# Two pad tensors between the buffers of a two-block transformer kernel on one core: activations and their split forms begin at a multiple of 256 bytes

## The chip, the cores and the metric

The kernel runs on one core of a Trainium2 chip. The metric is the device time of one execution in microseconds, as the median of the runs. A core has five engines with instruction streams of their own: TensorE (rows PE for matmuls and PEld for weight loads), VectorE (DVE), ScalarE (ACT), GpSimd (POOL) and SyncE (SP), which issues the DMAs here. The memory of the core that the engines read is called SBUF; each of its 128 partitions holds a line of bytes, and every tensor of the kernel lies at one byte address that is the same in all partitions.

## The reference

`reference()` computes two transformer blocks, each of depth two, over 512 tokens of width 1024, in float32:

```python
# first block, twice
x = layer_norm(ALPHA * x + 0.5 * swiglu(x, w_in, w_out))      # 1024 -> 2 x 2816 -> 1024
x = layer_norm(ALPHA * x + mixer(x))     # mLSTM, then windowed attention
x = layer_norm(ALPHA * x + 0.5 * swiglu(x, w_in, w_out))
# second block, twice
h = h + concat(hgrn2(p), nsa(p)) @ w_out           # p = rms_norm(h) @ w_in
h = h + swiglu(rms_norm(h), w_ffn_in, w_ffn_out)   # 1024 -> 2 x 2816 -> 1024
def swiglu(x, w_in, w_out):
    gu = x @ w_in; g, u = gu[..., :D_FF], gu[..., D_FF:]
    return (silu(g) * u) @ w_out
```

There are thus six swiglu layers, and most of the arithmetic is in them.

## The kernel before

**Weights.** All weights come as 535 units of 128 x 1024 float32, fetched in order into four buffers `raw0..3` (`Chip.fetch`). Each unit is split into a high part, rounded to the fp32r format, by ScalarE (`Chip.hi`, L211, into `whi0..3`), and the rest, by VectorE (`Chip.lo`, L219, into `wlo0..3`). Activations are split likewise: `xh` and `xl`, each 8 blocks of 128 channels by 512 tokens. A product of weights and activations is three matmuls in fp32r: high by high, high by low, low by high.

**A matmul** has a stationary operand of 128 x 128, loaded by a weight load of its own, and a moving operand of 256 or 512 columns. In a row of the profile the moving operand stands first: `ps<-tz,whi` moves tz past whi.

**A swiglu layer** (`Ffn`, six of them, `hf`, `tz`, `es` and `fb` are its tensors) has these stages:

1. Blocks j = 0 to 3 of the 22 blocks of 128 hidden channels: whole products with 256 or 512 moving columns of `xh` and `xl`, stationary `whi` and `wlo` (`Chip.three`, L238 to L240).
2. Blocks j = 4 to 21 (`seven_t`, `product`, L792 to L794): seven products of half size take the place of eight. Each is 12 matmuls with 256 moving columns, so a block is 84 matmuls. Three of the seven move a quarter of the activations (`xh`, `xl`), four move a form of the tokens T1 to T4, a sum or difference of quarters, that lies in `tz`. The stationary operand is a form of the weights, made by VectorE (`sum_v`) in `es` and `fb` and split into `whi` and `wlo` (L892, L987). There are 18 such blocks in a layer, 108 in all, and 9072 of these matmuls.
3. The product with `w_out` (`Norm.tile_t`, L367 to L369): the weights move (512 columns of `whi` or `wlo`), and the stationary operand is a 128 x 128 piece of the hidden activations, split into the ring `tz` (`split_a`, `split_v`, L920, L927).

**The mixers** take tensors of their own in the bytes that `hf`, `tz`, `es` and `fb` have in the swiglu layers. Their projections either move `xh` and `xl` (L238 to L240) or move the weights with `xh` and `xl` stationary (`Chip.wide`, L246 to L248; L1269 to L1271; L2118 to L2120; L1653 to L1655), their output products move the weights (L367 to L369). The compression in the second block moves the weights past `nxh` and `nxl`, whose pieces have 62 columns (L2132 to L2134).

**Where tensors lie.** Tensors are laid out in the order in which they are declared, each start rounded up to 32 bytes. The starts in the built program, as the remainder by 256 bytes:

| tensors | remainder before |
|---|---|
| raw, whi, wlo, xr, xh, xl | 128 |
| res, tmp, rows, st | 192 |
| hf, tz, es, fb | 64 |
| mixers: q and k of all three, nv, hkq, hv, had, hao, nkc | 64 |
| nxh | 0 (its pieces: 0, 248, 240, ...) |

The pieces of xh, xl, whi, wlo and tz that one matmul reads begin at multiples of 512 bytes behind the tensor's start, so they have its remainder.

Of the kernel before, what the change touches and what calls it, by code (L numbers as in the profile page):

```python
# [7 lines left out]
P = 128  # L8
# [94 lines left out]
class Tally:  # L103
# [4 lines left out]
    def __init__(self, make):  # L108
        self.make, self.sems, self.value, self.n = make, {}, {}, {}
        self.known = False  # L110
# [53 lines left out]
class Chip:  # L164


    def __init__(self, nc, ctx, xin, xtin, wst, vec, row, tab, mats_in, gain, out):
        self.nc, self.xin, self.xtin, self.wst, self.vec, self.row, self.tab = nc, xin, xtin, wst, vec, row, tab
        self.mats_in, self.gain, self.out = mats_in, gain, out
        self.tally = Tally(lambda name: ctx.enter_context(nc.semaphore(name)))  # L170
        self.up, self.at, self.also = self.tally.up, self.tally.at, self.tally.also
        sb = self.sb = lambda name, shape, dt=F32, scope=ctx: scope.enter_context(nc.sbuf_tensor(name, shape, dt))
        self.ps = ctx.enter_context(nc.psum_tensor("ps", [P, 8, 512], F32))
        self.raw = [sb(f"raw{i}", [P, UT * P]) for i in range(NRAW)]
        self.whi = [sb(f"whi{i}", [P, UT * P], F32R) for i in range(NW)]
        self.wlo = [sb(f"wlo{i}", [P, UT * P], F32R) for i in range(NW)]
        self.xr = sb("xr", [P, 4, D])
        self.xh = sb("xh", [P, KD, T], F32R)
        self.xl = sb("xl", [P, KD, T], F32R)
        self.vc = sb("vc", [P, V_N])  # L180
        self.res = sb("res", [P, P])
        self.ident = self.res[:, :]
        self.tmps = sb("tmp", [P, 5, T])
        self.tmp = [self.tmps[:, i, :] for i in range(5)]
        self.z = [self.tmps[:, 2 * i:2 * i + 2, :].rearrange("p a n -> p (a n)") for i in range(2)]
        self.rows = sb("rows", [P, 2, D])
        self.st = sb("st", [P, 4, 24])
        self.n_units = wst.shape[0]
        self.freed, self.read = {}, {}
# [2852 lines left out]
```

How the kernel before makes its waits and increments, by code:

```python
    def hi(self, a, upto):  # L204
        while self.nhi <= min(upto, self.n_units - 1):
            u = self.nhi
            a.wait_ge(*self.at(f"raw{u % NRAW}", u))
            if u >= NW:
                a.wait_ge(*self.at(*self.freed.get(u, ("gemm", "unit", u - NW))))
            a.activation(self.whi[u % NW][:, :], self.raw[u % NRAW][:, :], COPY).then_inc(*self.up("whi", u))
            self.nhi += 1
# [1 line left out]
    def lo(self, v, upto):  # L214
        while self.nlo <= min(upto, self.n_units - 1):
            u = self.nlo
            v.wait_ge(*self.at("whi", u))
            v.tensor_tensor(self.wlo[u % NW][:, :], self.raw[u % NRAW][:, :], f32(self.whi[u % NW][:, :]), SUB).then_inc(*self.up("wlo", u))
            self.nlo += 1
# [1 line left out]
    def fetch(self, s, u):  # L222
        if u >= NRAW:
            s.wait_ge(*self.at(*self.read.get(u - NRAW, ("wlo", u - NRAW))))
        s.dma_start(self.raw[u % NRAW][:, :], self.wst[u, :, :]).then_inc(*self.up(f"raw{u % NRAW}", u, by=16))
# [23 lines left out]
    def project(self, t, u, b, ks):  # L250
        if 0 in ks:
            t.wait_ge(*self.at("wlo", u))
        for k in ks:
            ins = self.three(t, self.bank(b), u, k, self.xh[:, k, :], self.xl[:, k, :], k == 0, k == KD - 1)
            if k == KD - 1:
                ins.then_inc(*self.up("gemm", "unit", u))
# [23 lines left out]
    def scalar(self, a):  # L281
# [6 lines left out]
            if k == 5:  # L288
                c.hi(a, 1)
        a.wait_ge(*c.at("vcin"))
# [1 line left out]
    def vector(self, v):  # L292
# [5 lines left out]
            if k == 5:  # L298
                c.lo(v, 1)
        v.wait_ge(*c.at("vcin"))
```

## Time and profile before

| what | value |
|---|---|
| median of 3 runs | 3289.93 us (3289.71 to 3290.17) |
| the profiled execution, its own time | 3290.32 us |
| its span, first to last instruction | 3288.5 us |
| TensorE matmuls | 22750, busy 3197.6 us (97%) |
| VectorE busy | 2144.5 us (65%) |
| ScalarE busy | 1534.5 us (47%) |
| DMA | 331.55 MB, mean 101 GB/s |

Busy time counts an engine as busy when any of its instructions is under way. A matmul's duration in a row includes the way through the array, which overlaps with the next matmul; what one matmul costs in a chain is its pitch, the time from its start to the start of the next. The pitch can be read from the timeline: the starts of two matmuls, some places apart, and their number between.

### The profile page before, as it was taken

What the parts mean: (1) busy time and instruction counts of PE and PEld (TensorE: products, weight loads), DVE (VectorE), ACT (ScalarE), POOL (GpSimd) and SP (SyncE); (2) the same over time, 40 slices, a digit from 0 to 9 for tenths busy, and PEclk for the clock granted to TensorE, in tenths of its full rate; (3) what the DMA queues carried; (4) which work ended last, traced back from release to release, by engine and by line L of the source; (5) the groups of instructions that cost most, each with busy time, mean ns of one, the idle gap of its engine ahead of it and who ended that gap; (6) DMA issues with size and microseconds to landing.
All of it is one profiled execution on the core that took longest, in us unless ns stands there. A gap on an engine that the chain in (4) does not pass through costs nothing. (4 is left out here: it accounts for less than half of the span.)

```text
span 3288.5 us, 55994 instructions
## 1 busy us (share of the span) xinstructions
PE 3197.6 (97%) x22750; PEld 2829.6 (86%) x22750; DVE 2144.5 (65%) x3383; ACT 1534.5 (47%) x2651; POOL 136.3 (4%) x144
## 2 busy tenths in 40 slices
PE   9999999999999999999999988999999989999999
PEld 8998888899889988768998776779998767789987
DVE  6875544787577766447875766557774665567863
ACT  4553444355434543553554544444554444444553
POOL 0000111000000001000000100000000000000000
PEclk9999999999999999999999999999999999999999
DMA  4443222234323432112343221113442221123332
GB/s 177 133 141 114 94 71 86 79 129 144 122 86 114 141 117 98 52 65 84 129 142 117 89 77 59 34 65 112 133 142 96 97 65 53 40 87 113 139 125 71
DMA packets 104512, 331.55 MB, mean 101 GB/s; under 512 B 11264, under 2 KB 16640, under 8 KB 104256
## 3 DMA queue, kind: packets, MB, share of 16 engines
q1 hardware_dynamic: 104256, 327.96, 29.7%
q8 instruction: 182, 2.98, 0.4%
q14 instruction: 74, 0.61, 0.1%
HBM read 325.69 MB, written 2.23 MB: 100 GB/s over the span
## 5 line engine op out<-in xcount | busy, mean ns | idle before, releaser
L219 DVE TENSOR_TENSOR wlo<-raw,whi 128x1024 fp32r<-128x1024 f32 x319 | 388.0, 1225 | 441.7 <-ACT whi L211 441.2
L211 ACT ACTIVATE whi<-raw 128x1024 fp32r<-128x1024 f32 x319 | 334.0, 1054 | 391.2 <-PE ps L369 338.6
L792 PE MATMUL ps<-tz,whi 128*128 128x256 f32 x1728 | 479.9, 278 | 3.4 <-ACT tmp L964 3.4
L793 PE MATMUL ps<-tz,whi 128*128 128x256 f32 x1728 | 478.5, 277 | 0.0
L794 PE MATMUL ps<-tz,wlo 128*128 128x256 f32 x1728 | 477.7, 276 | 0.0
L369 PE MATMUL ps<-whi,tz 128*128 128x512 f32 x1056 | 416.0, 394 | 0.0
L368 PE MATMUL ps<-wlo,tz 128*128 128x512 f32 x1056 | 413.8, 392 | 0.0
L367 PE MATMUL ps<-whi,tz 128*128 128x512 f32 x1056 | 411.3, 390 | 0.0
L794 PE MATMUL ps<-xh,wlo 128*128 128x256 f32 x1296 | 365.7, 282 | 0.0
L792 PE MATMUL ps<-xh,whi 128*128 128x256 f32 x1296 | 365.3, 282 | 0.0
L793 PE MATMUL ps<-xl,whi 128*128 128x256 f32 x1296 | 364.3, 281 | 0.0
L238 PE MATMUL ps<-xh,whi 128*128 128x512 f32 (+1 forms) x936 | 332.8, 356 | 18.2 <-DVE wlo L219 10.8
L792 PEld LDWEIGHTS ps<-tz,whi 128*128 128x128 f32 x1728 | 325.3, 188 | 4.4 <-issue 4.4
L793 PEld LDWEIGHTS ps<-tz,whi 128*128 128x128 f32 x1728 | 325.3, 188 | 0.0
L794 PEld LDWEIGHTS ps<-tz,wlo 128*128 128x128 f32 x1728 | 324.7, 188 | 0.0
L240 PE MATMUL ps<-xh,wlo 128*128 128x512 f32 (+1 forms) x936 | 320.3, 342 | 0.0
L239 PE MATMUL ps<-xl,whi 128*128 128x512 f32 (+1 forms) x936 | 320.2, 342 | 0.0
L792 PEld LDWEIGHTS ps<-xh,whi 128*128 128x128 f32 x1296 | 246.1, 190 | 0.5
L794 PEld LDWEIGHTS ps<-xh,wlo 128*128 128x128 f32 x1296 | 246.3, 190 | 0.0
L793 PEld LDWEIGHTS ps<-xl,whi 128*128 128x128 f32 x1296 | 246.1, 190 | 0.3
L368 PEld LDWEIGHTS ps<-wlo,tz 128*128 128x128 f32 x1056 | 198.3, 188 | 45.1
L367 PEld LDWEIGHTS ps<-whi,tz 128*128 128x128 f32 x1056 | 198.3, 188 | 43.1
(348 smaller groups left out, 6417.9 us busy)
## 6 DMA issues: line engine op xcount, KB each, us to landing
raw<-in_w SPq DMA_DIRECT2D x535, 512.0 KB, 4.0
fb<-in_w SPq DMA_DIRECT2D x108, 256.0 KB, 2.6
rows<-in_row SPq DMA_DIRECT2D x15, 512.0 KB, 4.9
xr<-in_xt SPq DMA_DIRECT2D x4, 512.0 KB, 6.8
xr<-in_x SPq DMA_DIRECT2D x1, 2048.0 KB, 7.8
mn<-bounds SPq DMA_DIRECT2D x8, 256.0 KB, 4.4
out<-tmp SPq DMA_DIRECT2D x4, 256.0 KB, 3.0
out<-rows SPq DMA_DIRECT2D x4, 256.0 KB, 2.3
```

What stands on the lines that cost most here:

```text
L211: a.activation(self.whi[u % NW][:, :], self.raw[u % NRAW][:, :], COPY).then_inc(*self.up("whi", u))
L219: v.tensor_tensor(self.wlo[u % NW][:, :], self.raw[u % NRAW][:, :], f32(self.whi[u % NW][:, :]), SUB).then_inc(*self.up("wlo", u))
L238: t.matmul(out, wh, xh, start=first, stop=False)
L239: t.matmul(out, wh, xl, start=False, stop=False)
L240: return t.matmul(out, wl, xh, start=False, stop=last)
L367: t.matmul(b, xh[:, sl], wh, start=k == 0, stop=False)
L368: t.matmul(b, xh[:, sl], wl, start=False, stop=False)
L369: ins = t.matmul(b, xl[:, sl], wh, start=False, stop=k == self.k - 1)
L792: t.matmul(out, fh[:, sl], xh[:, k, :], start=first and k == 0, stop=False, skip_group_check=not first)
L793: t.matmul(out, fh[:, sl], xl[:, k, :], start=False, stop=False, skip_group_check=not first)
L794: ins = t.matmul(out, fl[:, sl], xh[:, k, :], start=False, stop=k == 3, skip_group_check=not first)
```

## The change

Two tensors that nothing reads or writes are declared, one of 128 bytes ahead of `xh` and one of 64 bytes behind `xl`. No instruction is added, removed or moved.

```diff
         self.xr = sb("xr", [P, 4, D])
+        sb("pad0", [P, 32])
         self.xh = sb("xh", [P, KD, T], F32R)
         self.xl = sb("xl", [P, KD, T], F32R)
+        sb("pad1", [P, 16])
         self.vc = sb("vc", [P, V_N])
```

What follows from the order of declaration: `xh` and `xl` go up by 128 bytes, everything behind them by 192. The remainders by 256 become 0 for `xh`, `xl`, `hf`, `tz`, `es`, `fb` and for the mixers' q, k and others that had 64; 128 for `res`, `tmp`, `rows` and `st`; 192 for `nxh`. `raw`, `whi`, `wlo` and `xr` stay at 128.

## Rows read from the trace of the kernel before

**Rows 1.** The page: share of the span of each engine, and the slices.
```profile
span 3288.5 us, 55994 instructions
PE 3197.6 (97%) x22750; PEld 2829.6 (86%) x22750; DVE 2144.5 (65%) x3383; ACT 1534.5 (47%) x2651; POOL 136.3 (4%) x144
PE   9999999999999999999999988999999989999999
PEclk9999999999999999999999999999999999999999
```

**Rows 2.** Groups by line and form: busy us, mean ns | idle before.
```profile
L792 PE MATMUL ps<-tz,whi 128*128 128x256 f32 x1728 | 479.9, 278 | 3.4 <-ACT tmp L964 3.4
...
L369 PE MATMUL ps<-whi,tz 128*128 128x512 f32 x1056 | 416.0, 394 | 0.0
...
L792 PE MATMUL ps<-xh,whi 128*128 128x256 f32 x1296 | 365.3, 282 | 0.0
...
L238 PE MATMUL ps<-xh,whi 128*128 128x512 f32 x488 | 203.8, 418 | 11.9 <-DVE xl L297 7.1 <-DVE wlo L219 4.6 <-ACT wv L1725 0.2
...
L238 PE MATMUL ps<-xh,whi 128*128 128x256 f32 x448 | 128.9, 288 | 6.3 <-DVE wlo L219 6.2
```

**Rows 3.** Timeline, PE, a product that moves tz: start us, us.
```profile
694.65 0.28 PE L792 MATMUL ps<-tz,whi 128*128 128x256 f32 x1
...
697.03 0.28 PE L792 MATMUL ps<-tz,whi 128*128 128x256 f32 x1
```

**Rows 4.** Timeline, PE, a product that moves xh and xl.
```profile
682.31 0.28 PE L794 MATMUL ps<-xh,wlo 128*128 128x256 f32 x1
...
683.51 0.29 PE L792 MATMUL ps<-tz,whi 128*128 128x256 f32 x1
```

**Rows 5.** Timeline, PE, 512 moving columns of xh and xl.
```profile
50.07 0.39 PE L238 MATMUL ps<-xh,whi 128*128 128x512 f32 x1
...
51.43 0.39 PE L238 MATMUL ps<-xh,whi 128*128 128x512 f32 x1
```

**Rows 6.** Timeline, PE, 512 moving columns of weights, tz stationary.
```profile
299.65 0.39 PE L367 MATMUL ps<-whi,tz 128*128 128x512 f32 x1
...
305.14 0.39 PE L367 MATMUL ps<-whi,tz 128*128 128x512 f32 x1
```

**Rows 7.** Timeline, PE, 256 moving columns of weights, xh and xl stationary.
```profile
450.38 0.28 PE L1271 MATMUL ps<-whi,xl 128*128 128x256 f32 x1
...
451.58 0.28 PE L1269 MATMUL ps<-whi,xh 128*128 128x256 f32 x1
```

**Rows 8.** Timeline, PE, weights moving, nxh and nxl stationary: first and last pieces.
```profile
1918.07 0.28 PE L2132 MATMUL ps<-whi,nxh 128*62 128x256 f32 x1
...
1919.36 0.28 PE L2134 MATMUL ps<-whi,nxl 128*62 128x256 f32 x1
...
1925.89 0.28 PE L2133 MATMUL ps<-wlo,nxh 128*62 128x256 f32 x1
...
1927.07 0.28 PE L2134 MATMUL ps<-whi,nxl 128*62 128x256 f32 x1
```

**Rows 9.** Timeline, PEld, chains of weight loads with short matmuls.
```profile
1971.31 0.97 PEld L2247 LDWEIGHTS ps<-nkc,nq 128*128 128x128 f32 x8
1834.55 1.86 PEld L430 LDWEIGHTS ps<-tmp,xr 128*128 128x128 f32 x16 [0.25 <-issue]
```

**Rows 10.** Timeline, PE, and line L1291: 512 columns at two cycles each.
```profile
447.85 1.02 PE L1291 MATMUL ps<-mq,mk 128*128 128x512 f32 x2
L1291 PE MATMUL ps<-mq,mk x32: 590/591/592, 401.6 to 518.4; 128*128 128x512 f32 x32
```

**Rows 11.** Timeline, DVE, one block of stage 2 and the next block's first row.
```profile
693.47 0.43 DVE L1037 SCALAR_TENSOR_TENSOR ps<-tmp,ps 128x256 f32<-128x256 f32 x1 [0.65 <-PE ps L794]
...
696.28 0.69 DVE L1023 TENSOR_TENSOR hf<-tmp,ps 128x512 f32<-128x512 f32 x1 [1.25 <-PE ps L794]
696.88 1.22 DVE L987 TENSOR_TENSOR wlo<-es,whi 128x1024 fp32r<-128x1024 f32 x1
...
703.23 0.43 DVE L1037 SCALAR_TENSOR_TENSOR ps<-tmp,ps 128x256 f32<-128x256 f32 x1 [0.65 <-PE ps L794]
```

**Rows 12.** Timeline, PE, the second product of the next block begins.
```profile
698.79 0.29 PE L792 MATMUL ps<-tz,whi 128*128 128x256 f32 x1
```

**Rows 13.** Windows, stage 2 of one layer: busy us (x instructions), granted clock.
```profile
652.00:820.00 168.00, 167.44 (x1440) 167.27 (x1439) 133.26 (x186) 90.16 (x139) 0.00 (x0) 1.00 0.40 136
```

**Rows 14.** Line L987 on DVE: duration ns min/median/max, by source.
```profile
L987 DVE TENSOR_TENSOR wlo<-raw,whi x108: 1218/1219/1226, 45.4 to 3143.5; 128x1024 fp32r<-128x1024 f32 x108
L987 DVE TENSOR_TENSOR wlo<-fb,whi x108: 1215/1216/1218, 62.2 to 3158.5; 128x1024 fp32r<-128x1024 f32 x108
```

## The prediction

> **What bounds the kernel now.** I read the page first. TensorE is busy 97% of the span, at full granted clock in nearly every slice, and VectorE is at 65% [rows 1]. The groups by line say what TensorE does: its long groups have hardly any idle time before them [rows 2]. But the busy time of overlapping matmuls says nothing of what one costs, so I went to the timeline for pitches. A stretch of the stage with the seven products is 168 us with 1440 matmuls and 0.6 us without one [rows 13]. What a matmul costs from start to start is thus what the kernel costs, and a change of addresses can act only there.
>
> **Pitches by place.** The granted clock is 1.00 in that stretch, the level of 2.4 GHz, so 256 columns at one per cycle are 106.7 ns and 512 are 213.3 ns. Read off the timeline:
>
> Moving tz (remainder 64), stationary whi or wlo (128): 2.38 us over 21 matmuls, 113.3 ns, 6.7 above the columns [rows 3]. Moving xh or xl (128), the same stationary operand: 1.20 us over 10, 120.0 ns, 13.3 above [rows 4]. 512 columns of xh or xl: 1.36 us over 6, 226.7 ns, also 13.3 above [rows 5]. Weights moving (128) with xh stationary (128): 1.20 us over 10, 120.0 ns [rows 7]. Weights moving with tz stationary (64), 512 columns: 5.49 us over 24, 228.8 ns, 15.4 above [rows 6]. Weights moving with nxh stationary, whose pieces lie at 0, 248, 240 and so on: 1.29 us over 11, 117.3 ns for the first pieces, 1.18 us over 10, 118 ns for the last [rows 8].
>
> Rows 3 and 4 are the same instruction, with the same stationary operand, in the same stage. They differ in the moving operand's place, and the excess is 16 cycles at remainder 64 and 32 cycles at 128: a quarter of a cycle for each byte past a multiple of 256, as if a stream began at the multiple and dropped what it did not need. It is 32 cycles at 512 columns as well, so it is paid once per matmul. I take this as my theory: the moving operand's remainder by 256 sets the excess, and at 0 it is gone.
>
> **A floor.** A matmul also needs its weight load. Chains with little to move show what a chain of loads costs: 8 loads span 0.97 us, less the last one's 0.19 that is 0.78 over 7; 16 span 1.86 us, 1.67 over 15: 111.4 and 111.3 ns [rows 9]. The stationary operands there lie at 64 and at 128, so this floor does not depend on their place between these. I take 111.5 ns for 256 columns. With 512 columns the load has room. The nearest row for a wide matmul free of the excess is L1291, which takes two cycles per column: two of them span 1.02 us, less one duration of 0.59 is 0.43 us against 0.427 of columns [rows 10]. So 1 to 3 ns remain, and I take 216 ns.
>
> **The change part by part.**
>
> 1. Stage 2 of the swiglu layers. VectorE repeats its block every 703.23 - 693.47 = 9.76 us [rows 11], and a block is 84 matmuls: 116.2 ns on average, transitions between the two kinds included. At 111.5 ns a block is 9.37 us. 9072 matmuls x 4.7 ns = 42.6 us less. Bounds: at 113.3, if zero is no better than tz's 64, 26.3 us less; at the columns alone, 106.7, 86.2 us less, which the loads' floor excludes if it holds for this format too.
> 2. Moving xh and xl with 256 columns outside stage 2: 3 x 448 = 1344 matmuls [rows 2], 120.0 to 111.5: 11.4 us less. Bounds: 9.0 and 17.9.
> 3. Moving xh and xl with 512 columns: 3 x 488 = 1464 [rows 2], of which the first 48 of the kernel wait for their data anyway, so about 1416 x 10.7 = 15.2 us less. Bounds: nothing, and 13.3 each or 18.8.
> 4. Weights moving past tz (stage 3), 3 x 1056 = 3168 [rows 2, 6]. The moving side stays at 128, so its 13.3 stay. The stationary side goes from 64 to 0. At 128 it costs nothing on top (226.7), at 64 it costs 2.1. At 0 it may cost nothing (6.6 us less) or, if it grows with the distance, 4.2 (6.6 us more). I take no change. The other wide matmuls that move weights, 1152 of them, have xh stationary at 128 and go to 0: nothing, or up to 4.2 ns, 4.8 us more. The 62-column pieces go down from 0 by 8 bytes each to 136 and show no excess that follows their place [rows 8]; I take zero here too.
> 5. VectorE and ScalarE read and write the moved tensors. Source at 128 and at 64 give 1219 and 1216 ns for the same operation [rows 14]; nothing. The fp32 matmuls of the mixers pay about 1 to 5 ns at any remainder; nothing.
>
> Would another engine take over in stage 2? VectorE waits 0.65 + 1.25 = 1.90 us in a block of 9.76 [rows 11], so its own work needs 7.86 us and a block of 9.37 covers it. Its tightest hand-over is the second split: gate at the end of a product, 0.69 and 1.22 us, done at 698.10, needed by the second product of the next block at 698.79 [rows 11, 12]. Two products lie between, which shrink by some 0.1 us. The cover holds, and would be gone only near 8.6 us a block.
>
> The sum: 42.6 + 11.4 + 15.2 = 69.2 us less. The profiled execution itself took 3290.32 us for a span of 3288.5; its time is 0.4 us above the median, so both bases give the same: 3221.
>
> **A rule that speaks against it.** The Trainium skill, "SBUF — State Buffer", section "SBUF: two separate sides", says that TensorE's reads never wait for another engine; by that the places would not matter and the time would stay. Rows 3 and 4 differ by 6.7 ns with nothing else changed, so if it holds for other engines, TensorE's own two streams are still sensitive to place. "TensorE: Matmul & The Clock Gate" of the Trainium skill, section "Wait — 56ns, not 53.3ns?", has a fixed 2.5 ns on top of the columns whatever the addresses: 109.2 and 215.8 ns as an estimate. The wide figure fits my 216; the narrow one would give 9072 x 7.0 + 1344 x 10.8 + 16 = 94 us less, 3196, but rows 9 put the loads above it.
>
> **Rivals.**
>
> *Partial (0.17).* Zero is as good as 64 but no better: 26.3 + 9.0 + 1416 x 6.7 = 9.5, 45 us less: 3245. For it: rows 3 are only 1.8 ns above the loads' floor, so they don't prove that 64 costs 16 cycles rather than something else. Against: the round 16 and 32.
>
> *Mutual distance (0.09).* What costs is that the two streams lie at the same remainder; 128 apart, both are free, whichever moves. Then the matmuls that move weights gain as well: 3168 x 12.8 + 1152 x 10.7 + 1632 narrow ones x 8.5 = 67 us on top: 3154. Against it: the stationary pieces of nxh go from 128 apart from the moving weights to 8 apart, at 117 and 118 ns [rows 8].
>
> *Period of 128 (0.09), the one on the other side.* The excess depends on the remainder by 128, so 0 is as bad as 128, and tz had the best place. Then xh and xl stay at 120 and tz joins them: a block becomes 84 x 120 = 10.08 us, 0.32 x 108 = 34.6 us more; stage 3's stationary side gets 6.6 back: 28 us more, 3318. For it: no fp32r row moves anything at 0. It decides if the moving tz shows 117 ns or more.
>
> *Nothing (0.06).* The difference of rows 3 and 4 comes from something other than the start, such as the strides or the far address: 3290.
>
> **How the numbers follow.** My forecast has 0.59, the others as given. The likeliest one's own range is 3200 to 3236: less 11 us for the stationary side and a floor at 113 in part, more for a floor near 109. A measurement here tells 0.2%, 6.6 us, from no change. The range for 8 in 10 takes in the partial case and leaves out most of mutual distance and both on the other side: 3180 to 3262. Faster: 0.59 + 0.17 + 0.09 = 0.85; within 0.2%: 0.06; slower: 0.09.
>
> **What the profile of the changed kernel would show.** A product moving tz and one moving xh at the same pitch, 111 to 112 ns, and no transitions between them; VectorE's block at 9.37 us, its waits for TensorE shorter by 0.39; L238 with 512 columns at 216 ns; stage 3 at 227 to 231. The prediction is wrong if the moving side's place is not what made 113 and 120, if a stationary operand at 0 costs stage 3 more than 4 ns a matmul, or if the loads' floor is another one with whi at 128 than in rows 9.

## The result and the profile after

The changed kernel takes 3329.17 us in the median of 4 runs (3326.75 to 3329.40), the kernel before in the same comparison 3290.05 us (3289.71 to 3290.61). The ratio is 1.0117, with a 95% interval of 1.0100 to 1.0135: the change costs 39 us. The forecast was 3221 us, 69 us less than before.

The head of the page and two groups by line of the changed kernel; lines behind the pads are two higher, so L794 to L796 were L792 to L794, and L369 was L367.

```profile
span 3327.6 us, 55994 instructions
PE 3237.2 (97%) x22750; PEld 2851.6 (86%) x22750; DVE 2144.8 (64%) x3383; ACT 1534.5 (46%) x2651; POOL 136.7 (4%) x144
```

```profile
L794 PE MATMUL ps<-tz,whi 128*128 128x256 f32 x1728 | 486.7, 282 | 3.4 <-ACT tmp L966 3.4
...
L794 PE MATMUL ps<-xh,whi 128*128 128x256 f32 x1296 | 364.7, 281 | 0.0
```

The instructions are the same, and no idle time came up in front of these matmuls; VectorE and ScalarE are as busy as before [rows 1, 2]. In mean duration the matmuls that move tz went from 278 to 282 ns. The pitch says more. The timeline of TensorE in the changed kernel, in pairs of rows that are 21, 10, 24 and 24 matmuls apart: moving tz, moving xh, 512 columns of xh, and stage 3.

```profile
790.32 0.28 PE L794 MATMUL ps<-tz,whi 128*128 128x256 f32 x1
...
792.81 0.28 PE L794 MATMUL ps<-tz,whi 128*128 128x256 f32 x1
...
727.67 0.28 PE L794 MATMUL ps<-xh,whi 128*128 128x256 f32 x1
...
728.85 0.28 PE L795 MATMUL ps<-xl,whi 128*128 128x256 f32 x1
...
638.63 0.39 PE L240 MATMUL ps<-xh,whi 128*128 128x512 f32 x1
...
644.23 0.39 PE L240 MATMUL ps<-xh,whi 128*128 128x512 f32 x1
...
852.61 0.40 PE L369 MATMUL ps<-whi,tz 128*128 128x512 f32 x1
...
858.19 0.39 PE L369 MATMUL ps<-whi,tz 128*128 128x512 f32 x1
```

In each pair the start of the second less the start of the first, by the number of matmuls between, is the pitch: 2.49 us over 21, 118.6 ns, where [rows 3] had 113.3; 118 where [rows 4] had 120.0; 5.60 over 24, 233.3, where [rows 5] had 226.7; and 5.58 over 24, 232.5, where [rows 6] had 228.8. VectorE, which waits for TensorE once in each block of stage 2 at this line, shows the block:

```profile
709.36 0.43 DVE L1039 SCALAR_TENSOR_TENSOR ps<-tmp,ps 128x256 f32<-128x256 f32 x1 [0.75 <-PE ps L796]
...
712.27 0.69 DVE L1025 TENSOR_TENSOR hf<-tmp,ps 128x512 f32<-128x512 f32 x1 [1.36 <-PE ps L796]
...
719.32 0.43 DVE L1039 SCALAR_TENSOR_TENSOR ps<-tmp,ps 128x256 f32<-128x256 f32 x1 [0.75 <-PE ps L796]
```

A block takes 9.96 us instead of 9.76 and VectorE waits 2.11 us in it instead of 1.90 [rows 11]. The granted clock was not lower. It is at 1.00 in the window of [rows 13] here too (the window begins some us earlier in the layer than it did before, so its counts don't compare):

```profile
652.00:820.00 168.00, 167.44 (x1397) 166.57 (x1396) 129.58 (x182) 86.34 (x133) 0.00 (x0) 1.00 0.37 131
```

**Is it the other engines?** VectorE and ScalarE read and write the moved tensors too and might get in TensorE's way. A stretch of the swiglu layer in which VectorE, ScalarE, GpSimd and the DMA do nothing answers that. Here it is in the kernel before and then in the changed one, each time as a window (busy time of PE, PEld, DVE, ACT and POOL, granted clock, DMA share, GB/s) and as two matmuls in it, 22 apart:

```profile
644.60:649.70 5.10, 5.10 (x24) 4.24 (x23) 0.00 (x0) 0.00 (x0) 0.00 (x0) 1.00 0.00 0
644.59 0.39 PE L240 MATMUL ps<-xh,wlo 128*128 128x512 f32 x1
...
649.57 0.39 PE L238 MATMUL ps<-xh,whi 128*128 128x512 f32 x1
```

```profile
649.60:654.80 5.20, 5.20 (x24) 4.20 (x23) 0.00 (x0) 0.00 (x0) 0.00 (x0) 1.00 0.00 0
649.59 0.40 PE L242 MATMUL ps<-xh,wlo 128*128 128x512 f32 x1
...
654.73 0.40 PE L240 MATMUL ps<-xh,whi 128*128 128x512 f32 x1
```

The 22 matmuls take 4.98 us and 5.14 us. With the trace's full digits that is 226.7 and 233.3 ns each, so the whole difference is there while nothing but TensorE works. In stage 3 it is the same: where VectorE and ScalarE are both idle, the mean pitch went from 228.8 to 232.6 ns. Moving tz, TensorE is never alone for long, but where only ScalarE works beside it the pitch went from 113.4 to 118.6. What is left are TensorE's own reads.

**Where the 39 us are.** The time from the start of each matmul to the start of the next, summed over the whole trace by what moves and what is stationary, after less before, waits included: tz moving, 5184 matmuls, +23.0 us (115.1 to 119.6 ns each); stage 3 with tz stationary, 3168, +10.6; 512 columns of xh, 1464, +3.7; weights moving past xh with 512 columns, 1152, +3.4; 256 columns of xh, 5244 (the 12 of L812 counted in), -3.5; all others together, +1.7. The sum is 38.9 us, and 33.6 of it are in the matmuls that have tz on one side. How far such a sum varies with nothing changed in the pitches can be seen below, where all tensors go up by 128: up to 1.7 us for one kind.

### The profile page after: what moved, and what is told of

It reads as the page before. It is cut to its first block and busy times, and to the rows that moved or that the text cites. A ratio compares the mean times of both kernels' runs of the same rounds, so it can differ in the third digit from the quotient of the medians.

```text
span 3327.6 us, 55994 instructions
## 1 busy us (share of the span) xinstructions
PE 3237.2 (97%) x22750; PEld 2851.6 (86%) x22750; DVE 2144.8 (64%) x3383; ACT 1534.5 (46%) x2651; POOL 136.7 (4%) x144
## 5 line engine op out<-in xcount | busy, mean ns | idle before, releaser
L794 PE MATMUL ps<-tz,whi 128*128 128x256 f32 x1728 | 486.7, 282 | 3.4 <-ACT tmp L966 3.4
L796 PE MATMUL ps<-tz,wlo 128*128 128x256 f32 x1728 | 486.3, 281 | 0.0
L795 PE MATMUL ps<-tz,whi 128*128 128x256 f32 x1728 | 486.2, 281 | 0.0
L369 PE MATMUL ps<-whi,tz 128*128 128x512 f32 x1056 | 417.7, 396 | 0.0
L794 PE MATMUL ps<-xh,whi 128*128 128x256 f32 x1296 | 364.7, 281 | 0.0
L796 PE MATMUL ps<-xh,wlo 128*128 128x256 f32 x1296 | 364.6, 281 | 0.0
L794 PEld LDWEIGHTS ps<-tz,whi 128*128 128x128 f32 x1728 | 325.2, 188 | 4.5 <-issue 4.5
L796 PEld LDWEIGHTS ps<-tz,wlo 128*128 128x128 f32 x1728 | 325.2, 188 | 0.0
L794 PEld LDWEIGHTS ps<-xh,whi 128*128 128x128 f32 x1296 | 243.9, 188 | 0.5
L796 PEld LDWEIGHTS ps<-xh,wlo 128*128 128x128 f32 x1296 | 243.9, 188 | 0.0
```

Source lines behind the costliest of these rows:

```text
L369: t.matmul(b, xh[:, sl], wh, start=k == 0, stop=False)
L794: t.matmul(out, fh[:, sl], xh[:, k, :], start=first and k == 0, stop=False, skip_group_check=not first)
L795: t.matmul(out, fh[:, sl], xl[:, k, :], start=False, stop=False, skip_group_check=not first)
L796: ins = t.matmul(out, fl[:, sl], xh[:, k, :], start=False, stop=k == 3, skip_group_check=not first)
```

## The experiments

All of them are the kernel before with other pads, so an edit is given by its pads and by the remainders by 256 that it makes (weights, xh and xl, tz and all behind it). Before is 128, 128, 64; the change is 128, 0, 0. Each ratio is to runs of the kernel before on the same chip. Of two theories at the start, M says that the distance between the two operands counts, A that the place of the moving one does.

**All tensors up by 128 (0, 0, 192).**

```diff
+        sb("padr", [P, 32])
         self.raw = [sb(f"raw{i}", [P, UT * P]) for i in range(NRAW)]
```

> One pad of 128 bytes ahead of raw: every tensor goes up by 128 bytes, so whi, wlo, xh and xl lie at remainder 0 by 256 and tz at 192, and all distances between tensors stay. Theory M (the distance between the moving and the stationary operand by 256 bytes sets the pitch): nothing changes, 3290 us, tz moving at 113.3 ns, xh moving at 120.0, wide matmuls at 226.7 and 228.8. Theory A (the place of the moving operand by 256 bytes sets it, with 0 as bad as in the changed kernel): xh moving at 119 with a spread instead of a fixed 120, wide ones at 232, some 3300 to 3330 us.

Measured: 3290.22 us, ratio 1.0001 (0.9992 to 1.0010). Timeline of TensorE in this kernel, moving tz, moving xh, and stage 3:

```profile
780.59 0.28 PE L793 MATMUL ps<-tz,whi 128*128 128x256 f32 x1
...
782.97 0.28 PE L793 MATMUL ps<-tz,whi 128*128 128x256 f32 x1
...
719.21 0.28 PE L793 MATMUL ps<-xh,whi 128*128 128x256 f32 x1
...
720.41 0.28 PE L794 MATMUL ps<-xl,whi 128*128 128x256 f32 x1
...
841.66 0.39 PE L368 MATMUL ps<-whi,tz 128*128 128x512 f32 x1
...
847.15 0.39 PE L368 MATMUL ps<-whi,tz 128*128 128x512 f32 x1
```

113.3, 120.0 and 228.8 ns, as before to the tenth. xh moves from a multiple of 256 here and costs the full 13.3 ns above its columns, so theory A, and with it the theory of the prediction, is false. A theory of places by themselves that repeats every 128 bytes would also see nothing in this run. It fails in the next ones: xh goes from 128 to 0, and its pitch with 512 columns from 226.7 to 233. Shifts of all tensors by less than 128 were not tried.

**xh and xl alone (128, 0, 64).**

```diff
+        sb("pad0", [P, 32])
         self.xh = sb("xh", [P, KD, T], F32R)
         self.xl = sb("xl", [P, KD, T], F32R)
+        sb("pad1", [P, 32])
```

> xh and xl go to remainder 0, as in the change, and tz and all behind it keep 64. The changed kernel shows tz moving at 119 ns (113.3 to 115 before) and xh moving at 118.7. Theory M: tz stays at 113.3 to 115, stage 3 stays at 228.8, only the matmuls with xh change: 1464 + 1152 wide ones by about 3 to 5 ns, 9 us more in all, narrow ones about 1 ns less, 5 us less: 3290 to 3298 us. Theory A says the same of it. A third one, that the total order of the tensors or their far address counts, would show tz changed as well.

Measured: 3306.56 us, ratio 1.0053 (1.0036 to 1.0070). More than either theory gave. Stage 3 stays, but tz moving does not, though its remainder and that of its weights did not change:

```profile
785.78 0.28 PE L794 MATMUL ps<-tz,whi 128*128 128x256 f32 x1
...
788.25 0.28 PE L794 MATMUL ps<-tz,whi 128*128 128x256 f32 x1
...
847.50 0.39 PE L369 MATMUL ps<-whi,tz 128*128 128x512 f32 x1
...
853.00 0.39 PE L369 MATMUL ps<-whi,tz 128*128 128x512 f32 x1
```

2.47 us over 21, 117.6 ns, and as steady as the 113.3 was: over all layers nine in ten of these pitches lie from 117 to 119 ns. tz did go up by exactly 256 bytes here, but that is not the reason: it went up by the same 256 in three kernels below ((128, 64, 64), xl alone and (128, 96, 64)), and there it is at 113.3. At one and the same distance there are two lasting rhythms. The slow one costs 12.7 us in this kernel, the sum over tz moving.

**tz and all behind it alone (128, 128, 0).**

```diff
         self.xl = sb("xl", [P, KD, T], F32R)
+        sb("pad1", [P, 48])
```

> xh and xl keep 128, tz and all behind it go to remainder 0. Both theories: tz moving at 119 ns instead of 114.5, 5184 x 4.4 = 23 us more, and stage 3 at 232 instead of 228.8, 10 us more: 3320 to 3325 us, that is most of what the change costs.

Measured: 3324.11 us, ratio 1.0109 (1.0094 to 1.0124), as expected: tz moving +23.5 us, stage 3 +10.7, and xh stays at 120.0 and 226.7. In its timeline tz moving, then stage 3:

```profile
790.94 0.28 PE L793 MATMUL ps<-tz,whi 128*128 128x256 f32 x1
...
793.43 0.28 PE L793 MATMUL ps<-tz,whi 128*128 128x256 f32 x1
...
853.31 0.39 PE L368 MATMUL ps<-whi,tz 128*128 128x512 f32 x1
...
858.88 0.40 PE L368 MATMUL ps<-whi,tz 128*128 128x512 f32 x1
```

This half of the change makes 34 of its 39 us. Stage 3's weights did not move either: here it is the stationary operand's place relative to them that changed the pitch.

**xh, xl and tz all at 64 (128, 64, 64).**

```diff
+        sb("pad0", [P, 48])
         self.xh = sb("xh", [P, KD, T], F32R)
         self.xl = sb("xl", [P, KD, T], F32R)
+        sb("pad1", [P, 16])
```

> xh and xl go to remainder 64, where tz lies, 64 below the weights. Theories M and A: xh moving falls from 120.0 to 113.3 ns in narrow matmuls (5232 of them, 30 to 35 us less, and the transitions between tz and xh vanish, some 5 us less), wide ones with xh moving or stationary go from 226.7 to about 229 (2600 of them, 6 us more): 3255 to 3265 us. A theory in which tz is fast for another reason than its place would leave xh at 120 and the time at 3290.

Measured: 3261.55 us, ratio 0.9915 (0.9900 to 0.9929), faster than both kernels. tz has gone up by 256 bytes in all and keeps its 113.3. In its timeline moving xh, then 512 columns of xh:

```profile
712.46 0.28 PE L794 MATMUL ps<-xh,whi 128*128 128x256 f32 x1
...
713.60 0.28 PE L795 MATMUL ps<-xl,whi 128*128 128x256 f32 x1
...
626.61 0.39 PE L240 MATMUL ps<-xh,whi 128*128 128x512 f32 x1
...
632.21 0.39 PE L240 MATMUL ps<-xh,whi 128*128 128x512 f32 x1
```

xh moving falls to 1.14 us over 10, 114 ns (29.1 us less over all), and the transitions between the two kinds are gone (tz 4.3 us less). With 512 columns it rises from 226.7 to 233.3 (8.1 us more): what is the best place for 256 columns is a bad one for 512. That was expected at 229, from stage 3; but there the weights move past tz and lie 64 above it, here xh moves and lies 64 below. The sign counts.

**Other distances.** Three more layouts, each with two new ones: (128, 96, 32), (128, 192, 160), (128, 224, 192), by pads ahead of xh and behind xl of 56 and 0, 16 and 8, 24 and 8 elements.

> xh and xl at remainder 96, 32 below the weights' 128; tz and all behind at 32, 96 below. A theory of two kinds of place (a distance that is a whole number of 64-byte pieces or not): both get the same narrow pitch. A theory of a smooth dependence between the known points (0: 120.0, 64 below: 113.3, 128: 119): xh at 116 to 117 and tz at 116, time about 3290. If 64 below is a sharp optimum, both are at 119 to 120 and the time is above 3300.

> xh and xl at 192, 64 above the weights; tz and all behind at 160, 32 above. If only the size of the distance counts: xh moving at 113.3 ns as with 64 below, and wide ones as in rows of 64 below. If the sign counts (the stream that is ahead): xh near 119 to 120. Stage 3 then has the weights 32 below tz: between 226.7 (distance 0) and 232 (distance 128).

> xh and xl at 224, 96 above the weights; tz and all behind at 192, 64 above, so that in stage 3 the moving weights lie 64 below tz. A sign that counts: tz moving in stage 2 slower than 113.3, and stage 3 other than the 228.8 of 64 above. Only the size: 113.3 and 228.8 as before, with xh at 116 to 119.

Measured: 3320.50 (1.0092, 1.0063 to 1.0121), 3297.52 (1.0026, 1.0014 to 1.0037) and 3334.23 us (1.0134, 1.0104 to 1.0163). In the first, the time is that of the sharp optimum, and the pitches, 118.1 and 117.4, lie between it and the smooth curve. In the second and third the sign counts, but 64 above is better than was expected of it, 115.2 for 119 to 120. Pitches from all runs, each the mean over the matmuls of one kind that follow at least twelve of the same, in ns:

| moving less stationary, bytes | 256 columns | 512 columns |
|---|---|---|
| 0 | 120.0 | 226.7 |
| -32 | 118.1 | 233.3 |
| +32 | 116.7 | 233.3 |
| -64 | 113.3 to 113.9, or 117.7 | 233.3 |
| +64 | 115.2, or 117.8 | 228.9 to 230.3, or 233.0 |
| -96 | 117.4 | 234.2 |
| +96 | 120.0 | 233.3 |
| 128 | 118.7 | 232.4 to 232.9 |

For 512 columns the same place as the stationary operand is best and all others cost 2 to 7.5 ns, most of them 6 or 7. For 256 columns the same place is the worst or nearly so, and 64 below, in its fast rhythm, is the best. At 0 every run that has this distance shows the same fixed pitch; at 128 the pitch with 256 columns wanders between 115 and 122.

**wlo alone, xl alone.** In a triple the first and second matmul have whi stationary, the third wlo; while the second runs, wlo is loaded. These two ask which pair of operands it is that collides. (The first pad moves xr with wlo; both leave the remainder of tz at 64.)

```diff
+        sb("padw", [P, 16])
         self.wlo = [sb(f"wlo{i}", [P, UT * P], F32R) for i in range(NW)]
         self.xr = sb("xr", [P, 4, D])
+        sb("pad0", [P, 48])
```

> wlo alone goes 64 bytes up to 192; whi, xh, xl at 128, tz at 64. In each triple the first and second matmul have whi stationary and the third wlo; while the second runs, the load of wlo for the third runs. Theory N (the moving stream collides with the load for the next matmul, which runs under it): the second matmul of a triple changes, in wide ones of xh and xl L239's successor in pitch, from 226.7 to 229 to 233, L238 and the last one stay. Theory O (a matmul depends on its own stationary operand): the third changes and the second stays. In narrow ones moving xh a drop from 120 toward 113 for the one that changes. Time between 3285 and 3300.

```diff
         self.xh = sb("xh", [P, KD, T], F32R)
+        sb("padm", [P, 48])
         self.xl = sb("xl", [P, KD, T], F32R)
+        sb("pad1", [P, 16])
```

> xl alone goes to 64; xh, whi and wlo stay at 128, tz at 64. Only the second matmul of a triple has another distance (its own stationary whi and the load of wlo under it both 64 above the stream). This gives the lag between a matmul whose stream is moved and the row whose pitch changes: no lag, then in wide matmuls the pitch that starts at the xl row is the one near 233 to 236; a lag of one, then it is the wlo row's. With wlo moved alone the wlo row had 235.8. With a lag of one that points at the load of wlo under the second matmul's stream (theory N), with no lag at the third's own stationary operand (theory O). Time 3290 to 3320.

Measured: 3316.36 us (1.0080, 1.0050 to 1.0109) and 3284.57 us (0.9981, 0.9970 to 0.9991). The mean pitches with 512 columns, for the three of a triple in order, are 226.8, 226.6, 226.7 before; 228.4, 229.1, 235.8 with wlo moved; 229.3, 229.2, 228.4 with xl moved. The sum over a triple is 680, 693 and 687 ns, against 700 with all at 64. With wlo moved, 9.1 of the 13 ns stand at the third matmul; with xl moved the 7 ns are spread over all three. So neither theory N nor O is shown: it stays open whether the stream meets the load under it or a matmul depends on its own stationary operand. Both times lie outside what was expected. With wlo moved, the distance of tz to wlo changed as well, which the expectation left out: tz moving costs 20.4 us more and stage 3 9.9. With xl moved, xh and xl with 256 columns gain 8.0 us.

**xh and xl at 96, tz at 64 (128, 96, 64).** What leads tz into the slow rhythm?

```diff
+        sb("pad0", [P, 56])
         self.xh = sb("xh", [P, KD, T], F32R)
         self.xl = sb("xl", [P, KD, T], F32R)
+        sb("pad1", [P, 8])
```

> xh and xl at 96, tz and all behind at 64, 64 below the weights. With xh moved alone to 0, tz ran at a fixed 117.7 ns in its unchanged place, with xh at 128 or 64 at a fixed 113.3. Theory H (64 apart there are two lasting rhythms, 113.3 and 117.7, and the product before decides which one is taken; a product whose own pitch drifts, as xh does at 0 and at 96, leads into the slow one): tz at 117.7, time about 3305 to 3310. Theory K (only xh at a distance of 128 does that, for a reason of its own): tz at 113.3 to 114, xh at 117 to 118 as measured with 96 before, wide xh at 233.3: 3285 to 3290 us.

Measured: 3309.89 us, ratio 1.0069 (1.0052 to 1.0085). The time is theory H's, the pitches of tz, of xh (118.1) and of the wide matmuls of xh (233.3) are theory K's. In its timeline tz moving, then stage 3:

```profile
783.57 0.28 PE L794 MATMUL ps<-tz,whi 128*128 128x256 f32 x1
...
785.95 0.28 PE L794 MATMUL ps<-tz,whi 128*128 128x256 f32 x1
...
844.93 0.40 PE L369 MATMUL ps<-whi,tz 128*128 128x512 f32 x1
...
850.53 0.40 PE L369 MATMUL ps<-whi,tz 128*128 128x512 f32 x1
```

tz is at 113.3, so a drifting product ahead does not by itself bring the slow rhythm. But stage 3, with both operands at the remainders of the kernel before, is at 233.3 instead of 228.8, in all six layers, and costs 12.1 us. Its weights and tz lie at the very addresses that they have in the kernel (128, 64, 64), and there it costs what it did before. So the second rhythm exists with 512 columns too, and the distance by 256 bytes does not alone decide which one is taken. What does, these runs don't tell.

**Wide matmuls of xh cut in two.** With xh at 64 and, as a control, in the kernel before:

```diff
         wh, wl = self.w(u, j)
-        t.matmul(out, wh, xh, start=first, stop=False)
-        t.matmul(out, wh, xl, start=False, stop=False)
-        return t.matmul(out, wl, xh, start=False, stop=last)
+        n = xh.shape[-1]
+        for a in range(0, n, HT):
+            o, h, l = (x[:, a:a + HT] for x in (out, xh, xl))
+            t.matmul(o, wh, h, start=first and a == 0, stop=False)
+            t.matmul(o, wh, l, start=False, stop=False)
+            ins = t.matmul(o, wl, h, start=False, stop=last and a + HT >= n)
+        return ins
```

> As with xh, xl, tz all at 64, and each wide matmul of xh or xl past a weight is cut in two of 256 columns (1464 become 2928, with as many more weight loads). The wide ones cost 233.3 ns there, two narrow ones at 113.3 to 114 cost 227 to 228: 1416 x 5.5 = 8 us less than 3261.6, 3253 us. If the extra loads or instructions cost more than the columns, 3262 or above.

> The same cut in the kernel before, where xh and xl lie with the weights: two narrow ones at 120.0 take the place of one wide at 226.7, 13.3 ns x 1416 = 19 us more: 3309. It is the counterpart of the cut with xh at 64: the same edit with the other sign, by the place alone.

Measured: 3268.12 us (0.9941, 0.9924 to 0.9957) with xh at 64, the single runs from 3254.53 to 3274.33; 3302.88 us (1.0040, 1.0025 to 1.0055) in the kernel before. The profiled execution of the first was its fastest, 3254.53 us, and there the forecast is met; a stretch of the former wide matmuls in its timeline, ten apart:

```profile
601.04 0.28 PE L243 MATMUL ps<-xh,whi 128*128 128x256 f32 x1
...
602.18 0.28 PE L244 MATMUL ps<-xl,whi 128*128 128x256 f32 x1
```

114 ns each, 228 for a pair, against 233.3. The other runs are up to 20 us longer, and the median of all five is 6.6 us above the 3261.55 of the kernel with xh at 64 and no cut. No profile was taken of one of these; a change of rhythm would be of that size (4.2 ns over the 5184 matmuls that move tz are 22 us), but that is argued and not seen. In the control the same cut costs 13 us: two at 120.0 for one at 226.7. By the sums over its trace the cut matmuls cost 16.8 us more, near the forecast of 19, and all others together 5.6 less; why they do is open. One and the same cut is a loss with xh beside the weights and at best a gain with xh 64 below.

## Why the prediction was wrong

**The step that failed** is the sentence "I take this as my theory: the moving operand's remainder by 256 sets the excess, and at 0 it is gone". It drew a line through two points, 6.7 ns at 64 and 13.3 at 128, and read the third off it. The two kinds of matmul differ in the place of the moving operand, but with the weights fixed that is also a difference in distance, 64 and 0. Moving all tensors together separates the two: nothing changed, while xh moved from 0 at 120.0. What counts is where the moving operand lies relative to the stationary one (or to the one being loaded meanwhile: the runs with wlo and xl leave that open). The change put tz at a distance of 128, whether it moves or is stationary: 118.6 ns where the sum had 111.5, 232.5 where it had 228.8. And xh, at the remainder 0 that was to be free, has 118 and 233.3 where the sum had 111.5 and 216. Why a distance of 128 costs this much stays open.

**Rows 8 were read too widely.** They spoke against mutual distance because 62-column pieces showed none of it. That reading is right for these pieces: their median pitch is 117 to 118 ns in the traces of all fourteen kernels, wherever nxh lies. But their weight loads have 62 columns (rows of 0.13 us, against 0.19 with 128), and the matmuls with loads of 128 columns behave otherwise. The rows held no load of the kind that the sum was about.

**Point by point.**

1. The matmuls that move 256 columns of tz or xh, the first two terms: forecast 42.6 and 11.4, together 54.0 us less, measured 19.5 more (tz 23.0 more, xh 3.5 less). The block is 9.96 us, not 9.37.
2. 512 columns of xh: forecast 15.2 less, measured 3.7 more, outside the bounds, which held no loss.
3. Stage 3's stationary side: taken as nothing, bounds 6.6 either way, measured 10.6 more; the wide matmuls past xh 3.4 more, inside the bound of 4.8. The bound came from a straight line as well.
4. The floor of 111.5 ns was not reached by any layout: 113.3 is the least that 128-column loads with 256 columns moving showed in a steady stretch. Whether the loads set it is not shown.
5. VectorE and ScalarE don't feel the places: 2144.8 and 1534.5 us busy, against 2144.5 and 1534.5. That VectorE's cover holds was right, and shows in its longer waits.

**The rivals.** "Period of 128" was nearest in time, 3318, and its mark, tz at 117 or more, was met. Its reason is false: xh at 0 does not behave as at 128 (a wandering 118.7 for a fixed 120.0, 233.3 for 226.7 with 512 columns), and stage 3 lost where it was to gain. "Mutual distance" had the right quantity and the wrong curve: it took 128 apart to be free. "Partial" and "nothing" fell. The rule that the prediction set against itself is told more closely in another section of the same page: the Trainium skill, "SBUF — State Buffer", section "Who interferes with whom", has TensorE's moving operand and its weight load on independent read ports. Read as a rule on time, it would give all layouts the same time; here they go from 3261.55 to 3334.23 us with the same instructions. The measurement decides: whatever the ports are, the two operands are not independent of each other in pitch.

## What to carry to other kernels

Where TensorE is the bound and its operands are float32 words at one column per cycle, the distance by 256 bytes between the moving and the stationary operand is a parameter worth a scan, since pads cost nothing: here it moves the whole kernel by 2.2%. Read the pitch of each kind of matmul from the starts in the timeline, find the best distance for each column count by itself (64 below the stationary operand with 256 columns, the same place with 512), and expect a neighbour's change to show in matmuls whose own distance stayed. Two points in a trace are no curve, and before one operand's place is blamed, move both.

## What was not expected of the hardware

- The pitch of a matmul depends on the distance of its operands: 113.3 to 120.0 ns with 256 columns, 226.7 to 234.2 with 512, at the full granted clock, also while no other engine works. When all tensors lie 128 higher, nothing changes (3290.22 against 3290.26 us).
- The best and the worst distance change with the column count: 0 is the best with 512 columns, and the worst, beside +96, with 256.
- At a distance of 64 there are two lasting rhythms, 113.3 and 117.7 ns, or 228.9 and 233.0, held through all layers of a run. Which one is taken changes with places elsewhere, at the same remainders of the pair; by what way stays open.
